# Mixture-of-experts stages: a fifth pair of split buffers, one weight slab split ahead of the gather, and table zeros written one stage earlier

## The reference, cut to what matters

```python
def moe_ffn(x, w_router, b_router, w_gate, w_up, w_down):
    ...
    s = jax.nn.sigmoid((xt @ w_router).astype(jnp.float32))
    biased = s + b_router.astype(jnp.float32)
    grp_score = lax.top_k(biased.reshape(n, N_EXPERT_GROUPS, EXPERTS_PER_GROUP), TOP_K)[0].sum(-1)
    grp = jnp.argmax(grp_score, axis=-1)
    ...
    _, top_e = lax.top_k(jnp.where(in_grp, biased, NEG), TOP_K)
    w = jnp.take_along_axis(s, top_e, axis=-1)
    w = w / jnp.sum(w, axis=-1, keepdims=True)
    ...
    h = jax.nn.silu(jnp.einsum('nd,edf->nef', xt, w_gate)) * jnp.einsum('nd,edf->nef', xt, w_up)
    h = h * gate[:, :, None].astype(h.dtype)
    return jnp.einsum('nef,efd->nd', h, w_down).reshape(B, S, D)
```

## Time and profile before

| | |
|---|---|
| median of 3 runs | 2281.39 us (2280.94 to 2286.85) |
| the profiled execution | 2280.86 us, span 2279.1 us |
| PE busy | 2046.0 us (90%) |
| PEld busy | 1732.2 us (76%) |
| DVE busy | 1383.8 us (61%) |
| ACT busy | 949.9 us (42%) |
| POOL busy | 151.4 us (7%) |
| HBM read, written | 299.41 MB, 18.94 MB |

### The profile page before, as it was taken

How to read it: one execution, slowest core, us unless ns; L and a number is a source line. 1 busy time by engine, 2 the same in 40 slices (tenths; PEclk the granted TensorE clock), 3 DMA queues, 4 the chain that set the end, 5 groups by cost and what they waited for, 6 DMA issues and landing times. The chain is left out here.

```text
span 2279.1 us, 29889 instructions
## 1 busy us (share of the span) xinstructions
PE 2046.0 (90%) x11912; PEld 1732.2 (76%) x11912; DVE 1383.8 (61%) x1962; ACT 949.9 (42%) x1399; POOL 151.4 (7%) x209
## 2 busy tenths in 40 slices
PE   5999988969999898999979999699968887799995
PEld 5888878869999786776758888478957666688784
DVE  7864545545555454533468999745036675689896
ACT  5653335221000001623447777421125552477773
POOL 3442000000000000000020001000000000010010
PEclk9999998989999999999989999899879999799998
DMA  7433112214232223221249999432420002199993
GB/s 212 109 73 95 56 56 94 74 36 123 76 110 76 73 75 98 79 89 38 74 150 363 388 390 383 169 89 93 117 76 1 1 1 73 40 363 386 386 385 145
DMA packets 162200, 325.53 MB, mean 143 GB/s; under 512 B 30176, under 2 KB 98464, under 8 KB 161936
## 3 DMA queue, kind: packets, MB, share of 16 engines
q1 hardware_dynamic: 133872, 282.92, 35.4%
q0 software_dynamic: 11792, 32.33, 4.4%
q10 hardware_dynamic: 16400, 8.39, 1.5%
HBM read 299.41 MB, written 18.94 MB: 140 GB/s over the span
## 5 line engine op out<-in xcount | busy, mean ns | idle before, releaser
L2277 PE MATMUL ps<-m_ws,m_xbT 128*128 128x512 f32 x1344 | 317.8, 392 | 1.6 <-DVE m_ws L2515 1.6
L2277 PEld LDWEIGHTS ps<-m_ws,m_xbT 128*128 128x128 f32 x1344 | 254.0, 189 | 54.9 <-DVE m_ws L2515 1.8
L2515 DVE TENSOR_TENSOR m_ws<-ring,m_ws 128x2048 fp32r<-128x2048 f32 x112 | 255.8, 2290 | 38.2 <-ACT m_ws L2355 31.6
L1630 PE MATMUL ps<-ffT,ff_ws 128*128 128x264 f32 (+1 forms) x1056 | 241.7, 324 | 4.4 <-DVE ff_ws L433 4.4
L2355 ACT CAST m_ws<-ring 128x2048 fp32r<-128x2048 f32 x112 | 213.2, 1909 | 74.5 <-PE ps L2277 38.6
L1630 PEld LDWEIGHTS ps<-ffT,ff_ws 128*128 128x128 f32 x1056 | 176.9, 190 | 20.2 <-DVE ff_ws L433 4.5
L2319 PE MATMUL ps<-m_ws,m_hT 128*128 128x512 f32 x672 | 170.6, 404 | 0.0
L1630 PE MATMUL ps<-ffT_lo,ff_ws 128*128 128x264 f32 (+1 forms) x528 | 170.3, 323 | 0.0
L2319 PEld LDWEIGHTS ps<-m_ws,m_hT 128*128 128x128 f32 x672 | 124.4, 192 | 24.7
L2512 DVE TENSOR_TENSOR m_ws<-ring,m_ws 128x2048 fp32r<-128x2048 f32 x56 | 128.2, 2290 | 12.9 <-ACT m_ws L2353 12.3
L460 PE MATMUL ps<-fd_ws,fd_xs 128*128 128x512 f32 x528 | 121.9, 394 | 6.7 <-DVE fd_xs L433 6.7
(11 more groups left out here) (540 smaller groups left out, 4295.0 us busy)
## 6 DMA issues: line engine op xcount, KB each, us to landing
ring<-in_moe_w_gate SPq DMA_DIRECT2D x112, 512.0 KB
ring<-in_moe_w_up SPq DMA_DIRECT2D x112, 512.0 KB
ring<-in_moe_w_down SPq DMA_DIRECT2D x56, 1024.0 KB
ring<-in_w_up SPq DMA_DIRECT2D x22, 1024.0 KB
ring<-in_w_in SPq DMA_DIRECT2D x16, 1024.0 KB
ring<-in_gla_w_in SPq DMA_DIRECT2D x12, 1024.0 KB
ring<-in_w_down SPq DMA_DIRECT2D x11, 1024.0 KB
ring<-in_nsa_w_in SPq DMA_DIRECT2D x10, 1024.0 KB
```

Source lines behind the costliest of these rows:

```text
L1630: ins = nc.tensor.matmul(ps[:, bank, 0:b - a], w[j][:, k, s * P:(s + 1) * P], x[l][:, k, a:b], start=(k == 0 and j == l), stop=(k == KD - ...
L2277: ins = nc.tensor.matmul(ps[:, it % 2, :], xbT[:, blk % 2, a, 4 * half + k, :].bitcast(F32R), v[b][:, k, :], start=(half == 0 and k == 0 a ...
L2515: ins = V.tensor_tensor(o, x.rearrange("p (j k w) -> p j k w", k=4, j=2), x0, ALU.subtract)
```

## The change

`SPLITS` becomes 5, so a fifth pair of split buffers is there for both expert stages. Its room comes from the tile `rows`, which is now a view of `xT`. The rounded tokens move to pairs 3 and 4, so pair 2 is free from the start. `hi(2)` moves ahead of the gather's copies on ACT, and `lo(0)` ahead of the wait for the sigmoid on DVE; the later `hi` and `lo` each move up by one. POOL of m0 no longer writes zeros. Instead, POOL of the attention stage clears half of `xT` once `v` has been read, and writes the zeros from it: blocks 2 to 6 of `x_slots` (instead of all 7), the last two blocks of `y_slots` in one DMA, and `g_slots`. ACT of m0 waits for these seven DMAs (`zeros_in`) as its first act.

```diff
-SPLITS = 4
+SPLITS = 5
...
@@ gla_project, gpsimd
                 for to, frm in m["ln_loads"]:
                     pool.dma_start(to, frm).then_inc(self.ln_in, 16)
 
+                pool.wait_ge(o_done, N)
+                zero = m["xT"][:, 2:4].rearrange("p a c -> p (a c)")
+                nc.gpsimd.memset(m["xT"][:, 2:6], 0.0).then_inc(zeroed, 1)
+                pool.wait_ge(zeroed, 1)
+                for blk in range(2, NB):
+                    pool.dma_start(self.x_slots[P * blk:P * (blk + 1), :], zero).then_inc(self.zeros_in, 16)
+                pool.dma_start(self.y_slots[P * (NB - 2):P * NB, :].rearrange("(b p) d -> p b d", p=P),
+                               m["xT"][:, 2:6].rearrange("p (b a) c -> p b (a c)", b=2)).then_inc(self.zeros_in, 16)
+                pool.dma_start(self.g_slots.rearrange("(b p) e -> p b e", p=P), zero[:, 0:NB * EG].rearrange("p (b e) -> p b e", e=EG))\
+                    .then_inc(self.zeros_in, 16)
...
@@ moe_stage
-            rows = sb(ctx, tag + "_rows", [P, TT, D])
+            rows = xT[:].rearrange("p k c -> p (k c)").rearrange("p (t d) -> p t d", t=TT)
...
-            rh, rl = (ws[:, 2 + y].rearrange("p a (t c) -> p (a t) c", t=2) for y in range(2))
+            rh, rl = (ws[:, 3 + y].rearrange("p a (t c) -> p (a t) c", t=2) for y in range(2))
...
-            n_sent = 16 * (2 * TT + (NB + 3 if first else 0))
+            n_sent = 16 * 2 * TT
...
@@ scalar
+                if first:
+                    act.wait_ge(self.zeros_in, 16 * NB)
                 act.wait_ge(ones_set, 1)
...
                 round_x(2)
                 round_x(3)
+                hi(2)
                 act.preload_act_table(ACT.Silu)
                 for k in range(KD):
                     act.wait_ge(xp_done, k + 1)
...
-                hi(2)
                 hi(3)
+                hi(4)
...
@@ gpsimd
-                if first:
-                    nc.gpsimd.memset(xb[:, 0, :], 0.0).then_inc(zeroed, 1)
-                    pool.wait_ge(zeroed, 1)
...
-                    pool.wait_ge(sent, 16 * (NB + 3))
                 pool.wait_ge(slot_done, 1)
...
@@ vector
                 rest_x(0)
                 rest_x(1)
+                lo(0)
                 dve.wait_ge(loaded, 16 * len(loads))
                 dve.wait_ge(s_out, 1)
...
                 V.tensor_copy(slot[:], slotf[:]).then_inc(slot_done, 1)
-                lo(0)
                 lo(1)
+                lo(2)
...
-                lo(2)
                 lo(3)
+                lo(4)
                 dve.wait_ge(gw_done, 1)
```

More of the change, by code:

```diff
@@ L1818, in gla_project @@
             ybank = (0, 4, 6, 2)
-            centred = self.sem("gl_centred")
+            centred, zeroed = self.sems("gl", "centred", "zeroed")
+            self.zeros_in = self.sem("zeros_in")
             self.n_ln += 1
@@ L2455, in _ @@
             def _(pool):
-                if first:
-                    nc.gpsimd.memset(xb[:, 0, :], 0.0).then_inc(zeroed, 1)
-                    pool.wait_ge(zeroed, 1)
-                    for blk in range(NB):
-                        pool.dma_start(self.x_slots[P * blk:P * (blk + 1), :], xb[:, 0, 0:D]).then_inc(sent, 16)
-                    for blk in range(LAST, NB):
-                        pool.dma_start(self.y_slots[P * blk:P * (blk + 1), :], xb[:, 0, 0:D]).then_inc(sent, 16)
-                    pool.dma_start(self.g_slots.rearrange("(b p) e -> p b e", p=P), xb[:, 0, 0:NB * EG].rearrange("p (b e) -> p b e", e=EG))\
-                        .then_inc(sent, 16)
-                    pool.wait_ge(sent, 16 * (NB + 3))
                 pool.wait_ge(slot_done, 1)
```

## The result

The changed kernel takes 2270.72 us in the median (2267.83 to 2273.84, 6 runs) beside 2282.64 us of the kernel before (2280.94 to 2286.85, 6 runs, same chip). The ratio is 0.9947, with a 95% interval of 0.9933 to 0.9961: faster by 12 us, or 0.5%. Forecast were 4 us, with a range that ended at 2271.

What follows compares the result with a forecast made beforehand. The prediction took DMA engines, full all through the loop, and DVE's order behind the last landings to set each expert stage's end; 1.15 + 1.1 + 1.7 = 4.0 us off the 2281.39 median gave 2277.4 us, range 2275 to 2279.5, 8-in-10 range 2271 to 2282.

Steps and rivals of the forecast that it cites:

- The step that failed: Expert stages' end: full DMA engines set it, and PE's 3.39 and 3.98 us of waiting absorb its earlier losses or wins.
- depth brings nothing there: Loop behind unit 1: a fifth pair gains nothing, since PE never waited for a low part there.
- The sum: Whole kernel: 1.15 us (m0's tail), 1.1 (m1's tail) and 1.7 (clock kept in one tail) make 4.0 us saved.
- The lead: Loads in each expert stage: 1.9 us ahead to the end, as one slab moves in empty DMA time (2.6 less 0.7).
- The start: Router part: `lo(0)` delays the gather 0.7 us; unit 1 starts 0.6 us earlier in m0, 0.4 us later in m1.
- The reading of PE's waits: Loops of m0 and m1: apart from the few listed waits, PE's products were taken to run back to back.
- The slab's load: Start of m0: slab 5's load issued near 1177 instead of 1187.6, and slab 8's at 1205.1.
- The tail walk: Tails: last transposition 1.15 us earlier in m0 and 1.1 in m1, with 0.75 us of m0's gain lost to `rest_y(0)`.
- The clock in the tail: Last 24 products of each stage: lower clock costs 1.7 us; one of two tails counted as kept at full clock.
- The zeros: Moved from m0 to the attention stage: no gain and no wait, with 40 us of cover before ACT needs them.
- The slower case by ACT's queue: Rival: casts held by landings from block 4 delay later blocks' rows; 8.2 us slower, 2289.6 us; chance 0.08.
- The freed tail: Rival: landings come early enough that PE never waits in the tails; 11.0 us faster, 2270.4 us; chance 0.16.

Runs made afterwards that it cites:

- second profile of the kernel before: The kernel before, unaltered, profiled and timed once more: ratio 0.9999 to the kernel before.
- the second profiles: The kernel before and the changed kernel, both unaltered, each profiled and timed once more: ratios 0.9999 and 0.9944 to the kernel before.
- changed kernel with more work: Changed kernel with the 16 small products of the gates' table made twice in each expert stage: ratio 0.9998 to the kernel before.
- kernel before with more work: Kernel before with the 16 small products of the gates' table made twice in each expert stage: ratio 1.0034 to the kernel before.
- `rest_y(0)` early: Changed kernel with `rest_y(0)` moved on DVE from behind slab 83's low part to ahead of slab 81's: ratio 0.9948 to the kernel before.

## Why the prediction was wrong

**The step that failed** is the one on which its whole sum stood: "the end of the stage is set by the DMA engines, which have been full all through the loop", and with it "what PE loses or wins earlier in the loop is taken up by its 3.39 and 3.98 us of waiting at the end" and "depth brings nothing there". I read a DMA share of 1.03 as a bound. In place of this the runs showed that the last loads are asked for at PE's pace: the ring's requests follow the low parts, these the casts, these PE's reading. Less volume ahead of the last slabs gained nothing, 3 to 5 us more work of PE in a stage cost 7 to 12 us in all and, on the kernel before, left the waits at the end as they were (3.20 and 4.12 us), and the order of four pairs in loop and tail took back 10 of 12 us.

The waits of the casts alone would not have settled it. In the first pair of profiles most casts of the loop end their waits with PE. In the second profile of the kernel before, thirteen casts of m0 waited for DMAs up to 1269, up to 1.77 us, and PE had no wait for a product's operand behind them.

**The sum.** Its first two terms were the last transposition, 1.15 and 1.1 us earlier. Measured from the stage's start it was 3.90 us in m0 and 2.71 in m1, between the second profiles 3.15 and 1.40. The third was the clock behind it, 1.7 us; the last 24 products took 1.5 and 1.6 us less (m0, m1), between the second profiles 2.5 and 1.4. These terms add up to 9.7 us, where the two stages shrink by 9.6, and to 8.5 us of 8.7 between the second profiles. So the terms were the right ones, and their sizes followed from the step above.

**The lead.** Forecast 1.9 us; measured at slab 83's cast 4.4 us in m0 and 3.05 in m1, between the two repeats 3.5 and 1.7. So its size was off by up to a factor of two, and its cause was wrong. It isn't a slab moved in empty time: with `lo(0)` back behind the slots it is still there (4.2 and 2.9). The last request comes 3.6 us earlier by the fifth pair's place, and by as much more as PE is ahead (3.5 us in m0, 0.3 in m1, nothing in the repeats); 2.6 us of it in m0 and 0.8 in m1 are lost again between request and cast.

**The start.** Forecast 0.7 us later; the gather begins 25.38 us into m0 instead of 24.84, 0.5 us, and 0.4 in m1. Right. Unit 1 of m0 without a wait: right, at 42.17 instead of 43.80 us, 1.6 instead of 0.6 us earlier, since the gather took 9.78 instead of 10.52 us; that is not from the change, for in the second profile of the kernel before it took 10.03 and unit 1 began at 42.01. In m1 unit 1 came 0.2 us earlier, not 0.4 later. I gave no price to what stands in the earlier trace rows: the 24 products behind the wait took 7.34 and 7.36 us. This clock came back in both stages, 1.6 us each, in this pair of profiles; in the repeats there was nothing to come back.

**The reading of PE's waits.** "All else in the loops is products back to back" was not so: at the rows of later blocks PE waited 0.45 and 1.21 us in m0 and 0.63, 1.25 and 0.43 in m1, each ended by a DMA. The sum doesn't use them.

**The slab's load.** Slab 5's issue, forecast at 1177, came at 1173.39; both are 16.4 us into the stage. Right. The load of slab 8, forecast at 1205.1 (44.5 us in), was asked for at 1198.38 (41.4).

**The tail walk.** The loss by `rest_y(0)` was mis-sized: from cast 83 to the last transposition 5.94 us before and 6.44 after, 0.5 us instead of 0.75, in m1 0.34. The second last transposition as a place where the wait may go was seen ("unit 26's transposition needs `hT` 25"), but in m0 it took the whole wait, 2.54 us.

**The clock in the tail.** Forecast one of two kept. In this pair of profiles that came out, with the loss in another place: m1 kept it (5.74), m0 lost 1.4 us in the 12 products (4.38, where 12 of them take 2.98 at full clock). In the repeat both were kept, with waits of 0.97 and 1.46 in m0.

**The zeros.** Right as far as shown: alone 1.0009, taken back 0.9958, which lies within the interval of the changed kernel. ACT didn't wait for them at 1157.

**The rivals.** The slower case by ACT's queue did not come: in m0 casts waited for DMAs up to 1237 (1.63 us at the longest) and then not until slab 80, so at no later block; but PE got the new waits that deeper order brings, up to 1.44 us at unit 2's transposition. The freed tail named nearly the measured time (2270.4), but not the way: PE still waits 2.54 us in m0 and 1.40 in m1. That it comes so near the measured time is luck. The gain is shorter waits in the tail plus the clock behind them, and in the first pair of profiles also PE's start.

What stays open: how the 12 us divide in every execution, since the wait at unit 1 comes and goes; why start and depth bring more together than apart; and how much of the fifth pair's part is the earlier requests and how much the other order of the last slabs.

The Trainium skill's figure for HBM ("DMA: Bandwidth & Descriptors", section Specifications, about 358 GB/s for a core) was passed here again, with 390 GB/s over 180 us of the loop. No term that the runs left standing hangs on it.

## What to carry to other kernels

A full DMA share doesn't show that transfers set the pace; look at what ends the waits of the instruction that consumes them, in the middle of the loop and not only in the tail. Where two profiles of one kernel differ in that, as here, take bytes out or give the consumer more work. In this ring, the last request's time was the consumer's position less the depth, so a loss of the consumer early in a stage came out at its end, and one more place of depth moved the last request by one step of the loop (3.6 us), of which the queue took a part back. Then read the order of the last few items by itself: what only the final products need belongs behind everything that the ones ahead of them need, and this was worth 5 us on the changed kernel and 11 to 12 on the one before. And profile the unaltered kernel twice before explaining a difference of a few microseconds: here one of the two had a lower clock at unit 1 that the other had not.

## What the runs showed of the hardware

The granted clock fell behind small products without any wait: 32 products of four columns took 4.33 us (clock 0.82 from 1198.0 to 1202.5 in m0 of the changed kernel with more work), and the 24 large ones behind them 8.21 us (0.67 from 1202.5 to 1210.5), where 5.75 us is usual behind 16 small ones. After 16 small ones, a wait of 0.27 us was followed by 7.36 us in m1 of the kernel before, while in the tail, behind large products, waits of 0.96 to 1.46 us left the clock full (5.70 to 5.74 us) and one of 3.98 us did not (7.35 us). The length of a wait alone doesn't decide it. In m0 of the kernel before with more work a wait of 3.20 us was followed by 5.72 us. Ahead of 12 products, one of 2.14 us (`rest_y(0)` early, m0) was followed by 4.41 us and one of 2.76 us (changed kernel with more work, m1) by 3.00.

The DMA share was 1.02 at 390 GB/s and 1.00 at 378 to 380 GB/s, with 2.1 MB less to move; it hardly moved with the work to be done.
